# Fourier mixing over tokens: four quarter-length transforms of folded tokens in place of one product over all 512 rows

## What is computed

```python
def fourier_mix(u):
    B, N, _ = u.shape
    uh = u.astype(jnp.float32).reshape(B, N, FOURIER_HEADS, FOURIER_HEAD_DIM)
    y = jnp.fft.fftn(uh, axes=(1, 3), norm='ortho').real
    return y.reshape(B, N, FOURIER_WIDTH).astype(u.dtype)

    y = jnp.concatenate([fourier_mix(f_in), attn], axis=-1) @ w_out
```

## Time and profile before

| | before |
|---|---|
| median of 3 runs | 2358.28 us (2354.95 to 2360.48) |
| the profiled execution, whole | 2353.65 us |
| its span between first and last instruction | 2351.8 us |
| mean granted TensorE clock | 0.972 of full speed |
| TensorE busy (matmul records) | 2227.9 us, 95% |
| VectorE / ScalarE / GpSimd busy | 1081.7 / 757.3 / 87.5 us |
| read from memory | 231.96 MB |

### The profile page before, as it was taken

How to read it: one execution, slowest core, us unless ns; L and a number is a source line. 1 busy time by engine, 2 the same in 40 slices (tenths; PEclk the granted TensorE clock), 3 DMA queues, 4 the chain that set the end, 5 groups by cost and what they waited for, 6 DMA issues and landing times.

```text
span 2351.8 us, 25697 instructions
## 1 busy us (share of the span) xinstructions
PE 2227.9 (95%) x10940; PEld 1792.4 (76%) x10940; DVE 1081.7 (46%) x1450; ACT 757.3 (32%) x1134; POOL 87.5 (4%) x84
## 2 busy tenths in 40 slices
PE   6998999999994999999999999989999998999999
PEld 3666778888883788888888888776876676888887
DVE  3636665555537433334534333355375446443421
ACT  4314533222123322223332222223355635322211
POOL 0000000000001000000011100100000001111100
PEclk9999999999996999999999999989899998999999
DMA  7521136565620223332323322313200020333232
GB/s 262 191 82 59 64 126 192 187 194 176 202 94 29 89 91 98 98 99 94 95 91 93 104 89 92 102 56 117 72 2 1 1 90 19 107 91 107 85 99 85
DMA packets 190788, 236.64 MB, mean 101 GB/s; under 512 B 4097, under 2 KB 175393, under 8 KB 190545
## 3 DMA queue, kind: packets, MB, share of 16 engines
q1 hardware_dynamic: 189696, 230.42, 30.5%
q0 software_dynamic: 976, 4.57, 0.6%
HBM read 231.96 MB, written 2.10 MB: 100 GB/s over the span
## 4 chain that ended last, share of the span: by engine, by line
PE 88%; DVE 7%; ACT 3%; issue 1%; DMA 0%; POOL 0%; SPq 0%; DVEq 0%; ACTq 0%; POOLq 0%
PE ps L402 24%; PE ps L404 24%; PE ps L403 24%; PE ps L652 3%; PE ps L582 2%; PE ps L687 1%; PE ps L851 1%; PE ps L1001 1%; PE ps L468 1%; ACT pr L611 1%; PE ps L1982 1%; PE ps L2027 1%; DVE wl L351 1%; PE ps L381 1%; PE ps L446 1%
## 5 line engine op out<-in xcount | busy, mean ns | idle before, releaser
L402 PE MATMUL ps<-xh,wh 128*128 128x512 f32 x1800 | 713.9, 397 | 48.9 <-DVE xl L697 27.4
L403 PE MATMUL ps<-xl,wh 128*128 128x512 f32 x1800 | 706.4, 392 | 0.0
L404 PE MATMUL ps<-xh,wl 128*128 128x512 f32 x1800 | 706.4, 392 | 0.0
L351 DVE TENSOR_TENSOR wl<-raw,wh 128x2048 fp32r<-128x2048 f32 (+1 forms) x170 | 379.0, 2230 | 491.9 <-ACT wh L339 491.8
L402 PEld LDWEIGHTS ps<-xh,wh 128*128 128x128 f32 x1800 | 341.5, 190 | 128.7 <-issue 25.7
L339 ACT CAST wh<-raw 128x2048 fp32r<-128x2048 f32 (+1 forms) x170 | 314.5, 1850 | 340.1 <-PE ps L404 263.2
L404 PEld LDWEIGHTS ps<-xh,wl 128*128 128x128 f32 x1800 | 340.7, 189 | 73.0
L403 PEld LDWEIGHTS ps<-xl,wh 128*128 128x128 f32 x1800 | 341.5, 190 | 71.8 <-issue 1.2
L402 PE MATMUL ps<-hh,wh 128*128 128x512 f32 x704 | 274.1, 389 | 0.0
L404 PE MATMUL ps<-hh,wl 128*128 128x512 f32 x704 | 273.9, 389 | 0.0
L403 PE MATMUL ps<-hl,wh 128*128 128x512 f32 x704 | 273.9, 389 | 0.0
(11 more groups left out here) (329 smaller groups left out, 1799.0 us busy)
## 6 DMA issues: line engine op xcount, KB each, us to landing
raw<-in_ffn_w SPq DMA_DIRECT2D x52, 1024.0 KB, 5.4
raw<-in_ada_w SPq DMA_DIRECT2D x42, 1024.0 KB, 5.2
raw<-in_ffn_wg SPq DMA_DIRECT2D x22, 1024.0 KB, 5.4
raw<-in_ffn_wu SPq DMA_DIRECT2D x22, 1024.0 KB, 5.3
raw<-in_ffn_w SPq DMA_DIRECT2D x16, 896.0 KB, 4.9
raw<-in_ffn_wd SPq DMA_DIRECT2D x16, 896.0 KB, 4.8
raw<-in_w_in SPq DMA_DIRECT2D x10, 1024.0 KB, 5.2
raw<-in_ffn_wd SPq DMA_DIRECT2D x8, 1024.0 KB, 5.1
```

Of the source, the lines that this page charges most:

```text
L351: e.tensor_tensor(wl[s][:, 0:n], r[:, 0:n], wh[s][:, 0:n].bitcast(F32), ALU.subtract).then_inc(*WLO.up(i))
L402: e.matmul(dst, ah, bh, start=start, stop=False)
L403: e.matmul(dst, ah, bl, start=False, stop=False)
L404: return e.matmul(dst, al, bh, start=False, stop=stop)
```

## The change

Let x be the tokens of one head, in quarters x0 to x3 of 128 tokens. VectorE first makes, in `dve_fold`, for two heads at once, the differences x0-x2 and x1-x3, the sums x0+x2 and x1+x3 (in place), and of the two sums their sum and their difference. That is four tensor_tensor operations for two heads, eight in all: per pair of heads two of 512 elements per partition and two of 256. They stand in `dve_mix_in`, fold(0) ahead of the rotation of query chunk 0 and fold(1) ahead of those of chunks 1 and 2.

The output tokens t = 4r + s are then four groups s = 0 to 3, each with its own input of 128 folded tokens. For s = 0 and 2 it is real, so the product over dimensions is one matmul of 256 columns as before. For s = 1 and 3 it is complex (x0-x2 and the turned x1-x3), so there are two matmuls of 256 columns into the same bank. The transform over tokens then has, for each group s, a cosine and a sine product with 128 rows and 128 columns in place of 512, written to every fourth column of the PSUM bank. The number of matmul instructions of line 1001 stays 32; those of line 981 go from 16 to 24. The tables in `b1c` shrink from 5504 to 2688 columns per partition; a tile `folded` of 2048 columns is added. Copies out of PSUM, the four values of `ab` and the low and high parts are as before. TensorE waits once for each pair of heads for its fold.

```diff
-B1C = {"rot": 0, "cos": 128, "sin": 640, "cd": 1152, "cn": 1408, "sn": 1408 + 2048}
-NB1C = 1408 + 4096
+B1C = {"rot": 0, "cos": 128, "sin": 640, "cd": 1152, "cn": 1664, "sn": 1664 + 512}
+NB1C = 1664 + 1024
...
         qT = sb("qT", [P, 4, T], F32, part)
+        folded = sb("folded", [P, 4, T], F32, part)
...
+        def dve_fold(e, n):
+            x = fT[:, 2 * n:2 * n + 2, :]
+            y = folded[:, 2 * n:2 * n + 2, :]
+            e.wait_ge(*AE["in", 2 * n + 1])
+            e.tensor_tensor(y[:, :, 0:256], x[:, :, 0:256], x[:, :, 256:512], ALU.subtract).then_inc(*VF.up(("odd quarters", n)))
+            e.wait_ge(*VF["odd quarters", n])
+            e.tensor_tensor(x[:, :, 0:256], x[:, :, 0:256], x[:, :, 256:512], ALU.add).then_inc(*VF.up(("sums", n)))
+            e.wait_ge(*VF["sums", n])
+            e.tensor_tensor(y[:, :, 256:384], x[:, :, 0:128], x[:, :, 128:256], ALU.add).then_inc(*VF.up(("quarter 0", n)))
+            e.tensor_tensor(y[:, :, 384:512], x[:, :, 0:128], x[:, :, 128:256], ALU.subtract).then_inc(*VF.up(("folded", n)))
+
         def dve_mix_in(e):
             for n in range(1, 4):
                 dve_ahead(e, of["in", n])
                 if n > 1:
+                    dve_fold(e, n - 2)
...
         def pe_over_dims(e, c):
+            if c % 2 == 0:
+                e.wait_ge(*VF["folded", c // 2])
...
-                e.matmul(pb[5 + tb % 2][:, 0:256], fT[:, c, tb * P:(tb + 1) * P], b1("cd", 256), start=True,
-                         stop=True).then_inc(*ST.up(("dims", c, tb)))
+                dst = pb[5 + tb % 2][:, 0:256]
+                if tb % 2 == 0:
+                    m = e.matmul(dst, folded[:, c, 256 + tb * 64:384 + tb * 64], b1("cd", 256, P), start=True, stop=True)
+                else:
+                    e.matmul(dst, folded[:, c, 0:128], b1("cd", 256, P), start=True, stop=False)
+                    m = e.matmul(dst, folded[:, c, 128:256], b1("cd", 256, (tb - 1) * P), start=False, stop=True)
+                m.then_inc(*ST.up(("dims", c, tb)))
...
-                        m = e.matmul(pb[c % 2], ab[c % 2][:, tb, z * P:(z + 1) * P], b1(tab, T, tb * T),
-                                     start=tb == 0 and z == 0, stop=tb == 3 and z == 1)
+                        m = e.matmul(pb[c % 2].rearrange("p (s r) -> p r s", r=4)[:, tb], ab[c % 2][:, tb, z * P:(z + 1) * P],
+                                     b1(tab, P, tb * P), start=z == 0, stop=z == 1, skip_group_check=True)
```

More of the change, by code:

```diff
@@ L2418, in constants @@
     w = 2 * np.pi * (np.outer(r, r) % P) / P
-    b1[:, 1152:1280] = np.cos(w) / np.sqrt(P)
-    b1[:, 1280:1408] = np.sin(w) / np.sqrt(P)
-    w = 2 * np.pi * (np.outer(t, t) % T) / T
+    cd, sd = np.cos(w) / np.sqrt(P), np.sin(w) / np.sqrt(P)
+    b1[:, B1C["cd"]:][:, :512] = np.concatenate([-sd, cd, sd, -cd], 1)
+    w = 2 * np.pi * (np.outer(r, t) % T) / T
     cn, sn = np.cos(w) / np.sqrt(T), -np.sin(w) / np.sqrt(T)
-    b1[:, B1C["cn"]:][:, :2048] = cn.reshape(4, P, T).transpose(1, 0, 2).reshape(P, 2048)
-    b1[:, B1C["sn"]:][:, :2048] = sn.reshape(4, P, T).transpose(1, 0, 2).reshape(P, 2048)
+    b1[:, B1C["cn"]:][:, :512] = cn.reshape(P, P, 4).transpose(0, 2, 1).reshape(P, 512)
+    b1[:, B1C["sn"]:][:, :512] = sn.reshape(P, P, 4).transpose(0, 2, 1).reshape(P, 512)
     b2 = np.zeros((P, NB2C + 513), f)
```

## The result

The changed kernel takes 2339.85 us (median of four runs, 2336.13 to 2341.36) against 2356.61 us of before (median of four runs, 2354.53 to 2360.48): 16.8 us less by the medians. The ratio of the runs is 0.9925, 95% interval 0.9906 to 0.9943. Five more runs on another occasion gave 2339.08 against 2358.50 us, ratio 0.9922 (0.9910 to 0.9935), 19.4 us less. The forecast was 2342.8 us, that is 15.5 us less, with a range of 2337 to 2350.

What follows compares the result with a forecast made beforehand. TensorE's stream was taken to bound the Fourier stage. Its 15.9 us gain (41.6 to 25.7 us) less 0.4 us for the clock gave 15.5 us off the median 2358.28: 2342.8 us, range 2337 to 2350.

Steps and rivals of the forecast that it cites:

- What bounds it: Fourier stage: TensorE feeds everybody, busy 38.35 of 41.70 us, so time leaves where its stream gets shorter.
- The tokens' product, 20.1 us removed: Fourier stage: 32 products fall from 27.5 to 7.4 us, at 0.115 us a record, bound by weight loads.
- Exposed loads: Rival in the tokens' product: weight loads not hidden beneath moving columns, 7.1 us more, kernel 2348.8 us; chance 0.05.
- Dimensions, 3.4 us added: Fourier stage: 24 products over dimensions in place of 16, at 0.43 us each, add 3.4 us to TensorE.
- What takes over: Fourier stage: DVE's order matters, two TensorE stalls of 0.8 us and unit 15 at the end; 25.7 us for 41.6.
- the lay-out: Engines' programs of the Fourier stage side by side: 25.7 us after; 42.3 for the old kernel against 41.6 measured.
- The ada loads: Loads for DVE's ada units, 5.3 us each: unit 15's lands at 21.5, wanted at 22.5, one microsecond of slack.
- Folds and tables at nothing: DVE's two folds in mix_in, 4.4 us, covered by idle time and slack, cost 0; smaller table load worth 0.
- The clock, 0.4 us: Attention: more TensorE idle time beforehand brings a sooner or longer low-clock stretch, 0.4 us lost, bounds -0.5 and +2.
- a low clock within the stage: Rival: clock falls to 1.2 GHz in the Fourier stage, kernel 2357 us, or 2350 if half; chance 0.07.
- a slow strided output: Rival: tokens' product writing every fourth float of a PSUM bank at quarter rate, 2361.2 us; chance 0.04.
- Absorption: Rival: the stage shortens but a later stretch waits for something that doesn't move, 2358 us; chance 0.05.

Runs made afterwards that it cites:

- the width put back: Changed kernel with the tokens' product moving 512 columns again, with 128-row tables: stage 43.8 us against 24.8, kernel 2360.9 us in one run.
- the run with 64 columns: Changed kernel with the tokens' product moving 64 columns in place of 128: stage 24.6 us, kernel 2344.26 us in one run.
- the repeat: The changed kernel unchanged, timed again in the same rounds as the others: 2339.08 us (five runs) against 2358.50 of before, stage 24.8 us.
- contiguous output: Changed kernel with each group's 128 columns written to neighbouring floats of the PSUM bank: stage 24.8 us, kernel 2338.44 us in one run.
- one product over dimensions: Changed kernel without the second product over dimensions of the two complex groups: stage 22.6 us, kernel 2339.53 us in one run.
- no folds: Changed kernel with the folds left out, a tiny copy each keeping the wait: stage 24.8 us, kernel 2340.58 us in one run.
- double folds: Changed kernel with each fold done twice: stage 24.8 us, kernel 2340.57 us in one run.
- padded table: Changed kernel with the table tile padded back to 5504 columns, a 2752 KB load: stage 24.8 us, kernel 2335.97 us in one run.
- 23 filler products: Changed kernel with twelve unread TensorE products ahead of the attention and eleven behind its first scores: 2339.99 us in one run; the twelve alone 2337.91 us.

## Why the prediction was right, point by point

- **What bounds it.** TensorE's stream bounded the stage. Shown by the width put back: 19.0 us of the stage go with that one term.
- **The tokens' product, 20.1 us removed.** 64 records at 0.112 to 0.119 us are 7.2 to 7.6 us where 7.4 were forecast, from the attention's rows. The reason given, weight loads, is shown by the run with 64 columns. Exposed loads are ruled out: had load and columns followed each other, 64 columns fewer would have brought the records 0.05 us closer (half of the 0.107 us that 128 columns take at the pace of 0.43 us for 512), and they stayed 0.112 us apart. The rule that the prediction cites from the Trainium skill ("TensorE: Matmul & The Clock Gate", on what overlaps in packed matmuls), by which a load overlaps only a matmul of other row groups, does not hold for this stream.
- **Dimensions, 3.4 us added.** 48 records, as forecast. Their price in the stage is 2.2 us, with the narrow product (24.8 - 22.6) as with the wide one (43.8 - 41.6): the other 1.2 us fall into TensorE's waits for copies, which sum to 4.0 us without the eight added products and to 2.4 with them.
- **What takes over.** DVE's unit 15 set the end, and two stalls of 0.8 us stood where the lay-out put them. The stage was put at 25.7 us and took 24.8, just outside the 15.2 to 16.6 us of gain allowed for it (16.8) and just below the 25 to 27 us that the profile was to show. The lay-out charged a little too much at every turn. It had the modulation begin at 11.9 and it began at 11.3; the reader of head 0's tokens' product was put at 8.6 and came at 8.4; the last unit 15 began at 21.6 in place of 22.5. The same lay-out had given the old kernel 0.7 us too much, which was taken as an error of either sign and was one of one sign.
- **The ada loads.** The load of unit 15 was issued at 161.8 and landed 5.3 us later, at 167.1; the unit began at 167.8. The slack is 0.7 us, forecast 1.0.
- **Folds and tables at nothing.** Both shown, the folds while the weights are on time. The slack behind fold(1) was 2.1 us (124.81 to 126.96), not 1.3.
- **The clock, 0.4 us.** This term was mis-sized for the profiled pair, and the row under it was misread: a mean of 0.92 over 43.3 us with a low level of 0.5 is 6.9 us at the low level, not 3.5. The profiled execution was to take 2338.2 us and took 2341.36. The attention is 2.2 us longer (100.1 against 97.9) at 0.91 in place of 0.95. The spans differ by 12.2 us and not by 16.8: 16.8 less 1.2 in the prologue, 2.2 in the attention and 1.2 behind it. This pair stands at the two ends of the scatter, with mean clocks of 0.972 and 0.968, and between these the old kernel's own runs differ by 6 us and more (2353.83 against 2359.85 to 2361.37). The medians, which differ by 16.8 and 19.4, don't show the loss.
- **The attention as long as before within 2 us.** It was 2.2 longer. The changed kernel's 100.1 us is not chance: the repeat and five other traces with the same attention (contiguous output, one product over dimensions, no folds, double folds, padded table) have 99.7 to 100.1 us, all at 0.91. The kernel with the width put back had a long stage and still 0.93 and 99.7 us, so most of the loss does not hang on the short stage. Whether 97.9 us is typical of the kernel before is open: there is one trace of it.
- **The product of query chunk 2 at its old time within 0.2 us.** It came 1.2 us later, by the prologue; its distance from the one before it is the old 6.35 us.
- **The rivals.** Exposed loads, a low clock within the stage and a slow strided output are each excluded by a row. The stage idled 3.6 of 24.8 us, a larger share than the attention row that the prediction set against it (3.4 of 40), and was granted 1.00 all the same. Absorption did not occur in the medians. By its own parts the prediction's chances for within and slower are 0.07 and 0.03, not 0.06 and 0.04.

The right time owes something to the width of the range (13 us), and a little to errors of opposite sign: 0.9 us too small a gain in the stage against a clock term too small for the profiled pair. The large terms were right in themselves.

## What to carry to other kernels

Replacing a wide product by four narrow ones is worth its columns only down to the width at which a record costs its weight load; take that price from a row of the same shape elsewhere in the kernel. When the leading engine's share of a stage is halved, lay the other engines' programs beside it: here 1.4 us of the possible gain went to a unit of VectorE that had been hidden, and moving it elsewhere brought no gain that could be shown. Where whole times scatter by several us, measure the stage between two instructions, and compare whole times at equal granted clock.

## What was not expected of the hardware

Writing every fourth float of a PSUM bank costs a matmul nothing (24.8 us either way). And taking idle time away from TensorE only moved the low stretch of its clock: with 23 filler products the granted clock stayed at 1.00 for the attention's first 19 us, then fell, and the attention was as long as without them within 0.4 us (99.8 against 100.1, and 99.7 with twelve).
